# Head tiles of the input projection: the last tile's scaling and split go ahead of the next weights' split

## The reference, cut to what matters

```python
h = rms_norm(x, attn_norm_g[i])
proj = h @ w_in[i]
q, k, v, z, xbc, dt_raw = jnp.split(proj, splits, axis=-1)
# in dilated_attention: 8 query heads and 4 key heads of 64 channels
qh = rms_norm(q.reshape(bsz, seq, 4, 2, 64), q_g) * (64 ** -0.5)
kh = rms_norm(k.reshape(bsz, seq, 4, 64), k_g)
# rms_norm(x, g) = x * rsqrt(mean(x * x) + 1e-6) * g
```

## Time and profile before

| | us |
|---|---|
| median of 3 runs | 3023.37 |
| lowest and highest run | 3017.27, 3023.66 |
| the profiled execution's own time | 3030.15 |
| its span in the profile | 3028.4 |
| TensorE busy | 2917.8 (96%) |
| VectorE busy | 2000.0 (66%) |
| ScalarE busy | 1140.6 (38%) |
| DMA queue of GpSimd's stores, 60 to 240 us | 28.7% of 16 engines |
| DMA queue of SyncE, 60 to 240 us | 22.4% of 16 engines |

### The profile page before, as it was taken

How to read it: one execution, slowest core, us unless ns; L and a number is a source line. 1 busy time by engine, 2 the same in 40 slices (tenths; PEclk the granted TensorE clock), 3 DMA queues, 4 the chain that set the end, 5 groups by cost and what they waited for, 6 DMA issues and landing times. The chain is left out here.

```text
span 3028.4 us, 38640 instructions
## 1 busy us (share of the span) xinstructions
PE 2917.8 (96%) x14755; PEld 2304.8 (76%) x14818; DVE 2000.0 (66%) x2493; ACT 1140.6 (38%) x1735; POOL 282.3 (9%) x278
## 2 busy tenths in 40 slices
PE   8999999998989999899999999899999999999999
PEld 6788887875657566788778888788888788877887
DVE  7334555128566754545698899889998786776743
ACT  6321212112435354212254544544444444444321
POOL 0000000003434433000001000000000000000000
PEclk9999999998989999999999999999999999999999
DMA  4652222248675763643332244425542756443532
GB/s 149 202 161 77 62 81 68 63 110 202 170 203 150 192 176 99 209 142 115 140 112 77 98 146 160 174 94 193 191 149 104 257 199 229 145 155 120 188 115 66
DMA packets 260125, 435.04 MB, mean 144 GB/s; under 512 B 44049, under 2 KB 128529, under 8 KB 252913
## 3 DMA queue, kind: packets, MB, share of 16 engines
q1 hardware_dynamic: 255570, 408.32, 42.7%
q0 software_dynamic: 4384, 24.41, 2.2%
HBM read 312.18 MB, written 120.00 MB: 143 GB/s over the span
## 5 line engine op out<-in xcount | busy, mean ns | idle before, releaser
L103 PE MATMUL up_banks<-up_x_hi,up_w_hi 128*128 128x512 f32 x1232 | 484.9, 394 | 22.5 <-DVE up_x_lo L2734 7.0
L104 PE MATMUL up_banks<-up_x_lo,up_w_hi 128*128 128x512 f32 x1232 | 482.8, 392 | 0.0
L105 PE MATMUL up_banks<-up_x_hi,up_w_lo 128*128 128x512 f32 x1232 | 482.6, 392 | 0.0
L103 PE MATMUL inp_ps<-inp_h_hi,carry_q 128*128 128x512 f32 x896 | 353.7, 395 | 9.9 <-DVE inp_h_lo L200 9.8
L104 PE MATMUL inp_ps<-inp_h_lo,carry_q 128*128 128x512 f32 x896 | 350.4, 391 | 0.0
L105 PE MATMUL inp_ps<-inp_h_hi,carry_k_two 128*128 128x512 f32 x896 | 350.2, 391 | 0.0
L103 PEld LDWEIGHTS up_banks<-up_x_hi,up_w_hi 128*128 128x128 f32 x1232 | 233.3, 189 | 77.4 <-DVE up_w_lo L2667 16.0
L105 PEld LDWEIGHTS up_banks<-up_x_hi,up_w_lo 128*128 128x128 f32 x1232 | 233.3, 189 | 49.0
L104 PEld LDWEIGHTS up_banks<-up_x_lo,up_w_hi 128*128 128x128 f32 x1232 | 233.5, 190 | 48.5 <-issue 0.2
L2775 DVE SCALAR_TENSOR_TENSOR carry_rows<-carry_squares,up_conv_w,carry_rows 128x1024 f32<-128x1024 f32 x176 | 232.1, 1319 | 24.4 <-ACT carry_rows L2606 19.5
L103 PE MATMUL down_banks<-down_x_hi,down_w_hi 128*128 128x512 f32 x616 | 241.2, 391 | 7.0 <-DVE down_x_lo L2246 7.0
(11 more groups left out here) (384 smaller groups left out, 5321.4 us busy)
## 6 DMA issues: line engine op xcount, KB each, us to landing
carry_room<-in_w_up_dram SPq DMA_DIRECT2D x84, 512.0 KB, 4.4
act<-carry_rows SPq DMA_DIRECT2D x44, 512.0 KB, 2.9
carry_room<-cum_rows SPq DMA_DIRECT2D x16, 1024.0 KB, 6.7
carry_room<-x SPq DMA_DIRECT2D x7, 2048.0 KB, 9.1
carry_room<-in_w_in_dram SPq DMA_DIRECT2D x26, 512.0 KB, 6.0
xbc<-carry_room SPq DMA_DIRECT2D x12, 1024.0 KB, 5.7
carry_room<-xbc SPq DMA_DIRECT2D x16, 768.0 KB, 4.7
down_x<-act SPq DMA_DIRECT2D x12, 1024.0 KB, 7.3
```

What stands on the lines that cost most here:

```text
L103: pe.matmul(out, w_hi, x_hi, start=first, stop=False, skip_group_check=onto)
L104: pe.matmul(out, w_hi, x_lo, start=False, stop=False, skip_group_check=onto)
L105: return pe.matmul(out, w_lo, x_hi, start=False, stop=last, skip_group_check=onto)
```

## The change

On ScalarE and on VectorE the scaling, high part and low part of tile t - 1 are put ahead of the split of the weights of tile t + 2. On TensorE the sums by heads of tiles 3 and 4 stand ahead of block 4 of the next product, not block 3. SyncE's and GpSimd's programs are not touched.

```diff
@@ ScalarE, round t
                     act.wait_ge(evacuated, t + 1)
                     if t < QKT:
                         act.activation(qk_sq, stage[b], ACT.Square).then_inc(sq_done, 1)
-                    split(t, 0, b) if t % 2 == 0 else split(t - 1, 0, b)
                 if 0 < t <= QKT:
                     high(t - 1)
+                if t > 0:
+                    split(t, 0, b) if t % 2 == 0 else split(t - 1, 0, b)
                 if t < QKT:
                     take_head_root(t)
@@ VectorE, round t
                 if t > 0:
                     evacuate(t, b, stage[b])
-                    split(t - b, 0, b)
                 if 0 < t <= QKT:
                     kind = 0 if t - 1 < ATTN // P else 1
                     dve.wait_ge(inverse_in, 32 * t)
                     dve.scalar_tensor_tensor(out=stage[1 - b], in0=stage[1 - b], scalar=g_two[:, kind:kind + 1], in1=root,
                                              op0=ALU.mult, op1=ALU.mult).then_inc(normed, 1)
                     low_part(t - 1)
+                if t > 0:
+                    split(t - b, 0, b)
                 if t < QKT:
                     dve.wait_ge(folded, 32 * t + 32)
                     dve.reciprocal(fold[:, :], fold[:, :]).then_inc(inv_done, 1)
@@ TensorE (the loop runs once, for i = 1: products 4 and 5)
             for i in range(1, QKT // 2 - 1):
-                product(i * 2 + 2, 0, ps_free, lambda: add_up(i * 2 + 1, 1))
-                product(i * 2 + 3, 1, ps_free, lambda: add_up(i * 2 + 2, 0))
+                product(i * 2 + 2, 0, ps_free, lambda: add_up(i * 2 + 1, 1), None, 4)
+                product(i * 2 + 3, 1, ps_free, lambda: add_up(i * 2 + 2, 0), None, 4)
             product(QKT, 0, ps_free, lambda: add_up(QKT - 1, 1))
```

## The result

The changed kernel takes 3029.32 us (median of 13 runs, 3025.15 to 3035.01) against 3023.0 us for the kernel before (13 runs on the same chips, 3017.27 to 3028.41): a ratio of 1.0021, 95% interval 1.0013 to 1.0028, so 6.3 us slower (3.9 to 8.5). The forecast was 3.9 us slower. The profiled execution took 3033.77 us, with a span of 3032.0 where 3032.3 was forecast; that the two stand so close is partly luck, as will be seen. Some lines are numbered one or two higher than before: L686 is now L688, L694 is L696, L612 is L613, L561 is L562, L617 is L618, L637 is L639.

A forecast was written before the change was run, and what follows sets the result against it. TensorE was taken to bound the 3028.4 us span. Product 6's sums 1.9 us later plus 2.0 for the clock made +3.9 us: span 3032.3, median 3027.3, slower by 0.13%; 8-in-10 range 3019 to 3035 us.

The forecast's parts named there:

- What could be won: TensorE's stall at tile 3's sums in product 4: 6.35 us of wait plus 2.51 of clock, together 8.9 at most.
- The store chain: Evacuation through scaling, high and low parts, sorting and store: 24.0 us a round against TensorE's 23.01; 20 us after the change.
- (a): Low weights come behind the low part in round 1, so product 3 begins at about 90.6, 2.0 us later.
- (b): SyncE's queue: folds go behind the weight load that waits for the split, 4.8 us later against the low part's end.
- L: The time at which the low part ends in a round; forecast 89.36, 113.9, 138.4 and 163.0 in rounds 1 to 4.
- The new chain: Chain of the inverses, from low part through folds, write, broadcast and scaling to the next low part: 24.5 us a round.
- The clock: Lowered TensorE clock behind product 6's wait of some 4.2 us: costs 2.0 us, bounds 0 and 2.5.
- The sum: Product 6's sums start 1.9 us later, plus 2.0 for the clock: together +3.9 us, span 3032.3 us.
- Part 2: Sums of tiles 3 and 4 moved 12 matmuls, 2.7 us, later in products 4 and 5; costed at nothing.
- The faster rival: Chain of the inverses stays short, 21.9 us a round: 7.0 us gained, 3016.4; 6% whole, 10% for a part.
- the slower one: Folds also wait for the sorted store: round 27.1 us, product 6's sums 10 us late, 3035.4 us; 13%.
- The rival of lagging transfers: Folds to scaling takes 15.8 us as at tile 5: round 25.5 us, sums 4.7 late, 3030 us; 17%.

The follow-up runs named there:

- the late sums: Kernel before with only the sums of tiles 3, 4 and 5 moved ahead of block 6 of products 4 to 6: 0.9974 to before, again 0.9976.
- the load behind the folds: Changed kernel with SyncE still waiting for the split ahead of the folds, but the weight load issued behind them: 1.0021 to the kernel before.
- the second trace of the changed kernel: Trace from the changed kernel run again, unedited, beside one with only the changed order on ScalarE and VectorE: 1.0028 to the kernel before.
- the two pairs of runs: Changed kernel against the same with sums of tiles 3 and 4 back ahead of block 3: 1.0021 and 1.0010, then 1.0028 and 1.0014 to before.
- folds first: Changed kernel with SyncE's queue turned, folds issued ahead of the wait for the split and the weight load: 0.9994 to the kernel before.
- last sums late: Changed kernel with tile 5's sums ahead of block 6 of product 6 in place of block 3: 1.0005 to the kernel before.

## Why the prediction was right, point by point

- *What could be won* (8.9 us, 6.35 of wait and 2.51 of clock): right as a bound; the late sums won 7 to 8 of it.
- *The store chain is what held, at 24.0 us a round*: right. Moving one sum moved the wait along; moving three took it away.
- *(a), product 3 starts 2.0 us late, at 90.6*: measured 90.51, with a wait of 1.79 us. What I hadn't put in: behind so short a wait the granted clock fell too (0.72 from 90 to 96 us), and 60 matmuls took 105.94 - 90.51 = 15.4 us in place of 13.7. That is an event of this execution: in five of the seven traces in which product 3 waits it did not happen. It was hidden, since product 4 waited for its weights anyway.
- *(b), the folds behind the split's load, at L + 1.55*: measured L + 1.6 (116.86 against 115.27); shown to be the cause by turning the queue, and the wait rather than the 512 KB by the load behind the folds.
- *The new chain, 24.5 us a round*: right in kind, short in size. From folds to scaling it took 16.15, 16.33, 15.40 and 14.91 us in rounds 1 to 4, where I had 14.85 and an upper bound of 15.8. The folds are through at L + 7.1 to 7.2 in all four rounds (122.47 against 115.27 in round 2) where I had L + 6.3, but in rounds 3 and 4 that costs next to nothing, since the write lands with the sorted store as forecast: the broadcast is issued at L + 9.7 and 9.6 where I had L + 9.5. The mis-sized term is the landing of the write in rounds 1 and 2: the broadcast is issued at L + 10.6 and L + 11.0 (126.30). In round 1 the sorted store itself takes longer (the evacuation that waits for it starts at 99.78, L + 10.5); in round 2 the write comes 1.5 us behind the store (126.30 against 124.85), and why is not shown. The last two links were nearly as forecast: broadcast 6.9 to 7.3, scaling to low part 8.2. All this puts L of round 4 at 166.6 in place of 163.0, and these are the 3.6 us between the last sums' 180.3 and my 176.7.
- *The clock, 2.0 us*: 2.8 behind product 6's wait of 4.11, more than the bound of 2.5 that I had taken from a longer wait; 1.6 behind the same wait in the second trace of the changed kernel. One trace doesn't size this term.
- *The sum*: 3.9 forecast, 8.3 in the head tiles of the profiled execution, 6.3 in the median. The terms were too small by 4.4 (last sums 5.5 late in place of 1.9, clock 2.8 in place of 2.0), and the profiled span hides that, since the stages behind took 4.7 less. That the span came out at the forecast is luck.
- *Part 2 costs nothing*: not shown. It puts the waits into product 6, in front of a lowered clock; the two pairs of runs put 3 to 4 us on it, with overlapping intervals.
- *The faster rival* (a short chain) failed on the wait in SyncE's queue; *the slower one*, folds behind the sorted store, did not happen: they were through at 122.47 and the evacuation, which waits for that store, started at 124.85. In the other rounds too the folds were through 2.4 to 3.3 us before that evacuation. As the prediction read the Trainium skill's rule of turns (DMA: Bandwidth & Descriptors, "Queues, rings and completion order"), the store would have gone first; the trace doesn't agree with that reading in this position. *The rival of lagging transfers*, 25.5 us a round, describes what came best: the rounds' mean is 25.5.

## What to carry to other kernels

A reordering on two engines also reorders what a third engine's queue waits for: before moving an instruction, look for every in-order queue that waits on its semaphore, and at what stands behind that wait. Where a chain of another engine goes round more slowly than TensorE, a stall can't be removed at the place where it shows; it moves to the next point of contact, so all of these have to be moved: here that won 7 to 8 us, while the chain shortened by the folds first won nothing that shows against the kernel before. And moving TensorE's small dependent step later in its own program was worth more here, and took three numbers, than moving three instructions a round on the others.

## What the runs showed of the hardware

- A wait's length didn't decide alone whether the granted clock fell. Product 3 waited in seven traces: behind 1.79 and 2.30 us (last sums late) the clock was 0.72 in the next 6 us and 60 matmuls took 15.4 and 15.3 us, behind 2.14, 2.19, 2.20, 2.25 and 2.92 us it was 1.00 and they took 13.8 to 13.9. Two of these traces are of one kernel, the changed one; its second:

```profile
90.81 0.50 PE L103 MATMUL inp_ps<-inp_h_hi,carry_q 128*128 128x512 f32 x1 [2.20 <-DVE carry_k_two L613]
...
90.00:96.00 6.00, 5.19 (x23) 4.29 (x24) 0.76 (x1) 3.54 (x1) 1.00 (x2) 1.00 0.84 286
```

- The clock behind a wait of 4.11 us cost 2.8 us in one trace of the changed kernel and 1.6 in the other, behind 6.35 us 2.5 and behind 8.23 us 2.9, so the cost didn't grow with the wait.
- Two small folds (8 KB each) took 2.65 us with nothing ahead of them, 3.6 (load behind folds) to 4.15 with a 1 MB store ahead, and 5.6 with a store and a 512 KB load (116.86 to 122.47). Issued ahead of a store they were mostly not held by it, but the order of issue isn't the whole rule: in the last round of folds first, a store issued 1.1 us behind them (180.05), they took 5.8 us (178.98 to 184.80).
- The 1 MB broadcast took 6.9 to 7.3 us for rounds 2 to 5 of the changed kernel, with no store beside it, and 9.2 to 10.9 in folds first, beside a 1 MB store and with a weight load behind it.
